# Wide matrix products of a two-layer decoder kernel with moving weights and PSUM target addressed from the last column to the first

## The reference

```python
def swiglu_ffn(x, w_gate_up, w_down):
    gate, up = jnp.split(x @ w_gate_up, 2, axis=-1)      # 2048 -> 2 * 5632
    return (jax.nn.silu(gate) * up) @ w_down             # 5632 -> 2048

def reference(x, ...):
    h = x
    for layer in range(DEPTH):
        if layer < N_A_LAYERS:
            h = h + gated_deltanet(rms_norm(h, mixer_norm_g[layer]), ...)   # x @ w_in, chunked delta rule, @ w_out
        else:
            h = h + nsa_attention(rms_norm(h, mixer_norm_g[layer]), shared_kv, ...)
        h = h + swiglu_ffn(rms_norm(h, ffn_norm_g[layer]), ffn_w_gate_up[layer], ffn_w_down[layer])
        if layer == N_A_LAYERS - 1:
            shared_kv = nsa_shared_kv(h, kv_norm_g, kv_w, ...)              # kv_w, then compress_blocks
    return rms_norm(h, final_norm_g)
```

## Time and profile before

| | |
|---|---|
| time, median of 3 runs | 2810.07 us (2805.64 to 2810.47) |
| profiled execution, from first to last instruction | 2806.4 us |
| TensorE (matmul) busy | 2742.9 us, 98% |
| weight loads busy (beside the matmuls) | 2278.4 us, 81% |
| VectorE busy | 2220.1 us, 79% |
| ScalarE busy | 1651.4 us, 59% |
| granted TensorE clock, mean | 0.997 of full |
| DMA, mean | 176 GB/s |

### The profile page before, as it was taken

The page is one execution under the profiler, slowest core; times in us unless marked ns, Lnnn a source line. Parts: engine busy times, 40 slices in busy tenths (PEclk is TensorE's granted clock), DMA queues, the critical chain, the costliest instruction groups (busy, mean ns, idle before and its releaser), DMA issues.

```text
span 2806.4 us, 40252 instructions
## 1 busy us (share of the span) xinstructions
PE 2742.9 (98%) x13456; PEld 2278.4 (81%) x13456; DVE 2220.1 (79%) x2727; ACT 1651.4 (59%) x2184; POOL 31.0 (1%) x30
## 2 busy tenths in 40 slices
PE   8999999999988999999999999999999999999998
PEld 6878888888866888888888888888887888888887
DVE  5867977878776788888888876557677888888887
ACT  6766767667665555555555555554555555555554
POOL 0000000000000000000000000000000000000000
PEclk9999999999999999999999999999999999999999
DMA  6534444445433565555656556643345655556564
GB/s 239 180 130 148 165 147 161 160 137 175 147 111 112 168 213 198 189 191 197 201 195 201 199 171 224 221 135 113 106 155 200 203 199 195 201 180 200 196 201 165
DMA packets 135096, 493.23 MB, mean 176 GB/s; under 512 B 15008, under 2 KB 15328, under 8 KB 134624
## 3 DMA queue, kind: packets, MB, share of 16 engines
q1 hardware_dynamic: 133776, 487.82, 52.2%
q10 hardware_dynamic: 1232, 4.23, 0.4%
HBM read 489.86 MB, written 2.13 MB: 175 GB/s over the span
## 4 chain that ended last, share of the span: by engine, by line
PE 64%; issue 29%; DVE 3%; ACT 2%; DMA 2%; POOL 0%; POOLq 0%; DVEq 0%; SPq 0%; ACTq 0%
PE ACC L733 10%; PE ACC L735 10%; PE ACC L734 10%; PE SIDE L943 7%; PE SIDE L945 7%; PE SIDE L944 7%; PE ACC L945 3%; PE ACC L943 3%; PE ACC L944 3%; PE SIDE L741 2%; DMA RAW<-stream 2%; DVE W_LO L1627 1%; ACT W_HI L1194 1%; PE SIDE L1138 1%; ACT WORK L1587 0%
## 5 line engine op out<-in xcount | busy, mean ns | idle before, releaser
L1627 DVE TENSOR_TENSOR W_LO<-RAW,W_HI 128x1024 fp32r<-128x1024 f32 x424 | 511.7, 1222 | 268.2 <-ACT W_HI L1194 265.2
L1194 ACT ACTIVATE W_HI<-RAW 128x1024 fp32r<-128x1024 f32 x424 | 443.3, 1057 | 217.2 <-PE ACC L735 183.7
L1436 ACT ACTIVATE W_HI<-WORK 128x1024 fp32r<-128x1024 f32 x320 | 327.3, 1033 | 346.1 <-PE SIDE L945 234.1
L733 PE MATMUL ACC<-W_HI,X_HI 128*128 128x512 f32 x1216 | 489.6, 403 | 16.1 <-DVE W_LO L1627 16.0
L735 PE MATMUL ACC<-W_HI,X_LO 128*128 128x512 f32 x1216 | 475.3, 391 | 0.0
L734 PE MATMUL ACC<-W_LO,X_HI 128*128 128x512 f32 x1216 | 475.0, 391 | 0.0
L1878 DVE TENSOR_TENSOR W_LO<-WORK,W_HI 128x1024 fp32r<-128x1024 f32 x300 | 364.2, 1220 | 124.1 <-ACT W_HI L1436 124.1
L1436 ACT ACTIVATE W_HI<-RAW 128x1024 fp32r<-128x1024 f32 x328 | 315.5, 979 | 240.0 <-PE ACC L735 137.0
L733 PE MATMUL ACC<-W_HI,A_HI 128*128 128x512 f32 x928 | 370.7, 399 | 0.7 <-issue 0.7
L735 PE MATMUL ACC<-W_HI,A_LO 128*128 128x512 f32 x928 | 362.6, 391 | 0.0
L734 PE MATMUL ACC<-W_LO,A_HI 128*128 128x512 f32 x928 | 362.4, 391 | 0.0
(11 more groups left out here) (363 smaller groups left out, 3816.2 us busy)
## 6 DMA issues: line engine op xcount, KB each, us to landing
RAW<-stream SPq DMA_DIRECT2D x752, 512.0 KB, 4.5
WORK<-stream SPq DMA_DIRECT2D x160, 512.0 KB, 4.7
WORK<-gdn_rows ACTq DMA_DIRECT2D x8, 512.0 KB, 5.6
WORK<-xt SPq DMA_DIRECT2D x4, 512.0 KB, 9.0
H<-x SPq DMA_DIRECT2D x2, 1024.0 KB, 13.1
out<-WORK SPq DMA_DIRECT2D x4, 512.0 KB, 3.4
WORK<-tails SPq DMA_DIRECT2D x2, 512.0 KB, 10.8
WORK<-gfin SPq DMA_DIRECT2D x1, 1024.0 KB, 6.7
```

What stands on the lines that cost most here:

```text
L733: nc.tensor.matmul(dst, hi[:, at:at + P], wh, start=first and h % 2 == 0 and q == 0, stop=False)
L1194: nc.scalar.activation(W_HI[:, h % WS, :], raw_piece(h), ACT.Copy).then_inc(hi_ready, 1)
L1436: nc.scalar.activation(dst, src, ACT.Copy).then_inc(hi_ready, 1)
L1627: nc.vector.tensor_tensor(W_LO[:, h % WS, :], raw_piece(h), W_HI[:, h % WS, :].bitcast(f32), SUB).then_inc(lo_ready, 1)
```

## The change

A helper `down` turns an access pattern along its columns. In `products`, in `three` (and so in `up_products` and `last_products`) and in `compress_products`, the moving operand and the PSUM target are both turned. The stationary operands, the `start` and `stop` marks, the order of all instructions, the waits and the buffers stay. In the built program the last dimension of the two patterns goes from step 1 and offset 0 to step -1 and offset 511 (255 in the compression).

```diff
+        def down(ap):
+
+            return ap[:, ::-1]
+
         def products(pe, c, h, acc, hi, lo, first, last, base=0):
 
             pe.wait_ge(lo_ready, c + (h + 1))
             for q in range(2):
                 for t in range(NT):
-                    dst = ACC[acc][:, t * COLS:(t + 1) * COLS]
+                    dst = down(ACC[acc][:, t * COLS:(t + 1) * COLS])
                     at = (base + 2 * (h % 2) + q) * SEQ + t * P
-                    wh, wl = (b[:, h % WS, q * COLS:(q + 1) * COLS] for b in (W_HI, W_LO))
+                    wh, wl = (down(b[:, h % WS, q * COLS:(q + 1) * COLS]) for b in (W_HI, W_LO))
...
         def three(dst, hi, lo, wh, wl, start, stop):
 
+            dst, wh, wl = down(dst), down(wh), down(wl)
             nc.tensor.matmul(dst, hi, wh, start=start, stop=False)
             nc.tensor.matmul(dst, hi, wl, start=False, stop=False)
             return nc.tensor.matmul(dst, lo, wh, start=False, stop=stop)
...
-                    wh, wl = (b[:, h % WS, q * 256:(q + 1) * 256] for b in (W_HI, W_LO))
-                    d = SIDE[1][:, kv * COLS:kv * COLS + 256]
+                    wh, wl = (down(b[:, h % WS, q * 256:(q + 1) * 256]) for b in (W_HI, W_LO))
+                    d = down(SIDE[1][:, kv * COLS:kv * COLS + 256])
```

## The result

The changed kernel takes 2856.91 us (median of 4 runs, 2856.34 to 2860.76), before takes 2810.27 us (4 runs, 2805.64 to 2816.19). The ratio is 1.0175, with a 95% interval of 1.0163 to 1.0187. So it is slower by 1.75%, where no change was forecast; the time lies inside the stated range. The profiled execution has a span of 2859.0 us, 52.6 us over before's.

What follows compares the result with a forecast made beforehand. TensorE was taken as the bound; before's span of 2806.4 us plus 10512 x 0 and 128 x 0 stayed 2806.4 us, and with 3.7 us from span to median the forecast was 2810 us, range 2795 to 2925.

Steps and rivals of the forecast that it cites:

- What bounds the kernel: TensorE, busy for 2742.9 of 2806.4 us; in mid first FFN each nanosecond added to a wide product lengthens the kernel.
- The count and the split price: Wide products on TensorE: 10512 at 0.227 us make 2386 us; 0.426 ns a column plus about 9 ns fixed each.
- From one product to the next ... Cost: 0: Between successive wide products: same column order and 0.227 us distance, semaphore handovers of whole pieces unaffected; cost 0.
- The read order: Moving operand of each wide product read backward: cost taken as 0, since jumps between runs seemed free.
- the broken runs: Moving reads of two separate runs at lines 851 and 807: times equal to single-run reads, so jumps charge nothing.
- The write order: PSUM target of each wide product written backward: taken as 0, bounds -9 to +203 ns a product, less supported.
- The half rate: PSUM write or read of every wide product at two cycles a column: +203 ns each, about 4920 us; chance 0.19.
- The fixed charge: Start of each product, entered at its far end: 9 ns each, 95 us, time about 2905 us; chance 0.11.
- The gain: Weight load meeting the moving operand less often: 3 ns a product, 32 us, time about 2776 us; chance 0.05.
- The range and chances: Whole kernel: 2795 to 2925 us, holding about 0.78; faster 0.05, within 0.2% 0.65, slower 0.30.
- Slower: Whole kernel slower by more than 0.2%, 5.6 us: chance 0.19 + 0.11 = 0.30.
- the likeliest case: No change in the rate of wide products: time 2810 us, own range 2800 to 2818; chance 0.65.

Runs made afterwards that it cites:

- f1_pad_tr: Before with 128 unused bytes ahead of the buffers TR, UR, NR, YQ, all walks ascending: 2800.36 us, ratio 0.9973.
- f3_pad_x: Before with 128 unused bytes between the weight buffers and X_HI, all walks ascending: 2844.46 us, ratio 1.0133.
- e1_read_down: Changed kernel with only the moving operand walked downward, PSUM target upward, weight stream stored turned: 2856.55 us, ratio 1.0172.
- e5_widths: Changed kernel with 256 to 512 columns per product in `products`, upward or downward by piece, target upward; 2646.27 us in one run, columns left out.
- e3_halves_down: Changed kernel with moving operand and target walked as two ascending halves of a product, upper half first: 2808.27 us, ratio 1.0.
- e2_write_down: Changed kernel with only the PSUM target walked downward, moving operand upward, weight stream stored turned: 2808.87 us, ratio 1.0002.
- e4_pairs_down: Changed kernel with moving operand and target walked as 256 pairs from last to first, ascending within each pair: 2857.54 us, ratio 1.0179.
- e6_blocks: Changed kernel with `products` walked in backward blocks of 2 to 256 columns by piece, ascending within: 233.4 ns spacing at 2, 227.5 at 256.
- e7_shifts_up: In `products`, moving operand ascending but begun 1 to 128 columns further on by piece, wrong weights: mean spacing 236.7 ns at 1, 227.5 at 128.

## Why the prediction was wrong

**What bounds the kernel** held. TensorE is the bound, the loss lies on it alone, and a few nanoseconds per wide product went straight into the time.

**The count and the split price** held in part. 10512 products are right, and 52.6 us over them are 5.0 ns. But the spacing of 0.227 was read from one run of products and taken for all. Other stretches of the same trace, those with TR, UR, NR and YQ, read 0.233. Had I looked at a second place, I would have seen that a product's price depends on where its operands lie, and that 0.227 is a good case that can be lost.

**"From one product to the next ... Cost: 0"** was argued from distances in time and from semaphores alone, and didn't ask what the next product's weight load reads meanwhile. By the runs the spacing does depend on both operands' addresses (f1_pad_tr, f3_pad_x).

**The read order: the step that failed.** I took 0 because the broken runs of lines 851 and 807 cost nothing. The read alone costs about 6 ns per product of 512 columns, the whole loss (e1_read_down, ratio 1.0172). Those rows were too short to show it: 256 and 64 columns, and e5_widths finds no loss up to 320 columns even with each step backward. They are also plain float32 and run at half the rate: 256 columns in (1.89 - 0.38) / 7 = 0.216 us, against 0.118 for the float32r products, so a slower reader could hide there. Line 851 has one jump, and e3_halves_down shows that one jump is free at 512 columns too. The right row to bound it didn't exist in before, and the text said that no step but +1 was covered; the weight given to rows of other widths was too great.

**The write order** was called the less supported half. It costs nothing (e2_write_down), backward at every step.

**The rivals.** The half rate didn't happen. Of the two statements of the Trainium skill, the literal one of the page "PSUM — Partial Sum Buffer" (Specifications), that a non-contiguous pattern slows matmuls significantly, doesn't hold for a step of -1: ratio 1.0002. The other page of the Trainium skill, "SBUF — State Buffer" (its note on cachelines), counts hits on a line of 16 bytes in SBUF; for PSUM it only repeats the literal rule, so the prediction's "the same lines" joined two things. All walks of the changed kernel, e4_pairs_down and e6_blocks read the four columns of such a line one after the other and yet the short blocks cost the full 6 ns, so that count alone doesn't tell the read's price either. The fixed charge had the right side and size, +1 to +14 ns and a span of 2817 to 2954, but the wrong mechanism: it should show at 256 columns as at 512, and at 256 there is none. The gain was built on a meeting of the moving operand with the weight load. The two do depend on each other, by their addresses, but with the other sign: the ascending walk has the good case, and turning loses it.

**The range and chances.** Slower had 0.30 and the range held the time, yet the likeliest case was the wrong one. The range reached that far only for the sake of a fixed charge, which the runs refute, so that it held the time is luck.

## What to carry to other kernels

When a kernel is bound by a stream of equal matmuls, read the start-to-start interval for each pair of operand buffers, not once: differences of 3% between buffers are a placement that can be mended by idle bytes (here 128 of them, 8 us). For streams like these, put the two operands a multiple of 256 bytes apart. Let the moving operand ascend, or turn it in blocks of 128 columns or more; the PSUM target may be walked either way. Take a price for an access pattern from rows of the same width, since a short stream can hide what a long one pays.

## What the runs showed of the hardware

A float32r product of 512 columns with 128 stationary columns starts at best 226.7 ns after its predecessor at the full clock. It does so in runs in which the moving and the stationary operand begin at the same address modulo 512 bytes, and, once such a run has settled, also when they lie 256 bytes apart (e7_shifts_up; blocks of 32 on TR in e6_blocks). At other distances an ascending walk took 229.6 to 236.7 ns on X tiles. The sign counts too: with the moving operand 64 bytes ahead it was 229.6, with the stationary one 64 bytes ahead 233.1; at 128 bytes both gave 232.2. A walk of single backward steps took 233.3 to 236.2 ns at every distance tried. At 256 and 320 columns the direction made no difference (118 and 147 ns), and at 256 neither did the tile's address: the compression's tiles begin 480 bytes apart, and its median interval is 118 ns for all.

What the reader of the two operands does is not shown. Two things stay open: why the loss sets in between 320 and 384 columns, and whether the single backward step costs by itself or only by passing through all distances. A stationary operand walked the other way, which would tell these two apart, was not tried.
